# Attention: value products on the 64 columns of the unit's own head, and the results of a tile in one PSUM bank

## The reference, cut to what matters

```
s_loc = q @ k_window.T * scale (+ bias, mask);  s_ctx = q @ k_cache.T * scale
p     = softmax([s_loc, s_ctx] (, sink))
o     = p_loc @ v_window + p_ctx @ v_cache
```

## Time and profile before

| | |
|---|---|
| median of 3 runs | 4721.29 us (4719.97 to 4725.55) |
| profiled execution, its own time | 4717.61 us |
| its span, first to last instruction | 4715.8 us |
| mean granted TensorE clock | 0.906 |
| busy: PE, PEld, DVE, ACT, POOL | 3943.4, 3420.0, 1757.2, 866.7, 683.1 us |
| attention units, even layer | about 366 to 583 us |
| attention units, odd layer | about 2654 to 2922 us |

### The profile page before, as it was taken

The page is one execution under the profiler, slowest core; times in us unless marked ns, Lnnn a source line. Parts: engine busy times, 40 slices in busy tenths (PEclk is TensorE's granted clock), DMA queues, the critical chain, the costliest instruction groups (busy, mean ns, idle before and its releaser), DMA issues. The chain is left out here.

```text
span 4715.8 us, 62439 instructions
## 1 busy us (share of the span) xinstructions
PE 3943.4 (84%) x25842; PEld 3420.0 (73%) x25842; DVE 1757.2 (37%) x3337; ACT 866.7 (18%) x2008; POOL 683.1 (14%) x521
## 2 busy tenths in 40 slices
PE   4979978986769999996999597438886859999995
PEld 3976623444569999995999475338885659999995
DVE  3245541224531211123123454677876441121112
ACT  2113320001100110012111123424443100011001
POOL 2000110111100011002000000036651101001100
PEclk7988979997889999997999798768997979999998
DMA  4226412314547777773421402332223547777774
GB/s 151 89 82 233 148 67 98 137 40 149 201 148 268 261 266 264 268 257 117 116 89 67 108 8 76 102 88 60 73 65 130 190 154 264 268 259 267 266 268 155
DMA packets 353335, 744.94 MB, mean 158 GB/s; under 512 B 87432, under 2 KB 193559, under 8 KB 351976
## 3 DMA queue, kind: packets, MB, share of 16 engines
q1 hardware_dynamic: 333066, 683.15, 40.9%
q0 software_dynamic: 17392, 57.58, 4.5%
q10 hardware_dynamic: 2618, 0.40, 0.1%
HBM read 635.63 MB, written 106.10 MB: 157 GB/s over the span
## 5 line engine op out<-in xcount | busy, mean ns | idle before, releaser
L1826 PE MATMUL moe_b<-moe_xT,ffn_w 128*128 128x144 f32 x8192 | 1022.9, 287 | 0.0
L1826 PEld LDWEIGHTS moe_b<-moe_xT,ffn_w 128*128 128x128 f32 x8192 | 1012.7, 191 | 1.8
L1826 PE MATMUL moe_b<-moe_gu,ffn_w 128*128 128x144 f32 x4096 | 550.7, 288 | 0.0
L1826 PEld LDWEIGHTS moe_b<-moe_gu,ffn_w 128*128 128x128 f32 x4096 | 516.3, 190 | 4.8
L1871 DVE TENSOR_TENSOR moe_gu<-moe_sg,moe_b 128x144 f32<-128x144 f32 x256 | 77.9, 304 | 782.3 <-PE moe_b L1826 782.3
L1851 ACT ACTIVATE moe_yT<-moe_b 128x144 f32<-128x144 f32 x256 | 74.6, 291 | 1074.8 <-PE moe_b L1826 1074.8
L2380 PE MATMUL gdnc_a<-gdnc_T,gdnc_part 128*128 128x128 f32 x864 | 139.3, 318 | 156.7 <-POOL gdnc_part L2537 88.0
L1859 DVE TENSOR_SCALAR moe_xT<-moe_x,keep_coef 128x128 f32<-128x128 f32 (+1 forms) x544 | 154.7, 346 | 252.2 <-PE moe_x L1778 252.1
L2380 PEld LDWEIGHTS gdnc_a<-gdnc_T,gdnc_part 128*128 128x128 f32 x864 | 128.0, 229 | 162.7 <-POOL gdnc_part L2537 149.9
L1747 POOL DMA_INDIRECT scratch_x<-moe_ys,moe_slot x32 | 51.8, 1619 | 1260.7 <-DVE moe_yp L1881 1260.7
L297 PE MATMUL proj_mm<-proj_hT_low,proj_w_high 128*128 128x384 f32 x576 | 193.2, 335 | 0.0
(11 more groups left out here) (413 smaller groups left out, 6401.2 us busy)
## 6 DMA issues: line engine op xcount, KB each, us to landing
ffn_w<-moe_w_gate SPq DMA_DIRECT2D x32, 4096.0 KB, 15.8
ffn_w<-moe_w_up SPq DMA_DIRECT2D x32, 4096.0 KB, 13.9
ffn_w<-moe_w_down SPq DMA_DIRECT2D x32, 4096.0 KB, 15.7
attnrun_m_w<-w_ada SPq DMA_DIRECT2D x40, 1024.0 KB, 9.4
scratch_conv<-proj_zf POOLq DMA_DIRECT2D x24, 512.0 KB, 3.0
scratch_tm<-proj_tm SPq DMA_DIRECT2D x45, 208.0 KB, 1.9
proj_w_raw<-even_w_in SPq DMA_DIRECT2D x24, 384.0 KB, 4.2
scratch_spec<-filt_res SPq DMA_DIRECT2D x36, 256.0 KB, 2.1
```

The lines of the kernel that those rows point to most:

```text
L1826: mm = nc.tensor.matmul(bk[(m * FC + f) % 3][:, 0:SLOTS], w[m][:, k, f * P:(f + 1) * P], src[:, k, :], start=k == 0, stop=k == KD - 1)
```

## The change

The value tiles that stream are cut to the 64 columns of the unit's own head, in the keys' values (`tok`) and in the cached ones (`cv`). The result tensor `po` becomes 8 x 64 float32, one bank in place of two. Since the heads' results now lie side by side, VectorE scales all eight with one instruction of 512 elements in place of two of 256. The number, the order and the waits of TensorE's instructions stay.

```
-        po = s.ps("po", [P, 8, P])
+        po = s.ps("po", [P, 8, HD])
...
-            at = P * plan.kv_chunk(h)
-            tiles = [tok[:, k, v_at + at:v_at + at + P] for k in keys]
+            at = P * plan.kv_chunk(h) + HD * plan.chunk_half(h)[1]
+            tiles = [tok[:, k, v_at + at:v_at + at + HD] for k in keys]
             if cached:
-                tiles = [cv[:, at:at + P]] + tiles if even else tiles + [cv[:, at:at + P]]
+                tiles = [cv[:, at:at + HD]] + tiles if even else tiles + [cv[:, at:at + HD]]
...
-                for half in range(2):
-                    if even:
-                        src, r, dst = po[:, 4 * half:4 * half + 4, 64 * half:64 * half + 64], rinv[:, g % 2, 4 * half:4 * half + 4], o_sb[:, g % 2, 4 * half:4 * half + 4, :]
-                    else:
-                        src, r, dst = po[:, half:8:2, 64 * half:64 * half + 64], rinv[:, g % 2, half:8:2], o_sb[:, g % 2, half:8:2, :]
-                    ins = nc.vector.tensor_tensor(dst, src, r.unsqueeze(2).broadcast_to([P, 4, HD]), ALU.mult)
-                ins.then_inc(o_done, 1)
+                nc.vector.tensor_tensor(o_sb[:, g % 2], po[:], rinv[:, g % 2, :].unsqueeze(2).broadcast_to([P, 8, HD]), ALU.mult).then_inc(o_done, 1)
```

## The result

The changed kernel takes 4891.59 us, the median of four runs (4890.37 to 4892.26); beside them the kernel before took 4720.63 us (4719.85 to 4725.55, four runs). The ratio is 1.036 with a 95% interval of 1.0342 to 1.0378: slower by 171 us. The forecast was 4900, its range 4865 to 4918. The profiled execution of the changed kernel took 4892.26 us, with a span of 4890.5 and a mean granted clock of 0.866 (before: 0.906).

What follows compares the result with a forecast made beforehand. TensorE's pace and granted clock were taken to bound both attention stages. V 0, scaling 0, odd layer +176 and even layer +4 gave +180 on 4717.6, so 4897.6, forecast 4900 after the runs' median offset; range 4865 to 4918.

Steps and rivals of the forecast that it cites:

- V's length: V products in both layers: weight loads set their pace, so 64 columns save 0, bounds -68 us and 0.
- the bound of -68 us: V in both layers: the saving if the spacing of its 1216 records halved as the columns do, 68 us.
- the rival of cheap narrow products: V in both layers: 64-column records need half the time; 4653 us if the clock holds; chance 0.02 with clock kept.
- the ends of groups: Odd layer, TensorE's wait at seven group ends: 1.75 us each at half clock, +12.3, bounds 0.85 and 2.56 each.
- Bank and scaling: One bank and one VectorE scaling instruction for two: taken as 0, bounds -2.7 us and 0.
- The odd layer's clock: Odd layer stays at half clock to its end: tiles 0 to 7 take 419.4 us, +172.8; with the prompt +176.
- The prompt: Odd layer's last V block and prompt units, about half at full clock before: about +3 us.
- The even layer: Even layer: clock rises slightly later, +2 us, and may fall earlier in the prompt units, +2; sum +4.
- The clock holds: Rival, whole kernel: clock follows how long TensorE is occupied, so no change, 4721 us or 1 to 3 less; chance 0.08.
- Comes back in some groups: Rival, odd layer: full clock returns in one to seven groups, about 20 us saved each, 4880 to 4760; chance 0.09.

Runs made afterwards that it cites:

- experiment 1: Kernel before with only the V products narrowed to 64 columns in both layers, two banks and two scaling instructions kept: 4894.59 us.
- experiment 4: Changed kernel plus unread 512-column products in the odd layer: in set-up, first scores and group ends 4708.6 us; start only 4868.68; without set-up 4705.18.
- experiment 5: Changed kernel plus unread 64-column products, four in place of each 512-column one, behind the odd layer's first scores and at its group ends: 4916.0 us.
- Experiment 3: Kernel before with V streaming 96 or 80 of the 128 columns in both layers, two banks kept: 4765.48 us and 4870.44 us.
- experiment 4, start only: Changed kernel plus unread 512-column products in the odd layer, 35 in its set-up and 2 behind its first scores, none at group ends: 4868.68 us.

## Why the prediction was right

- *V's length: nothing.* Nearly. The spacing of the weight loads stayed at 0.21 us at half clock (eight in 1.78) and the same at full (four in 0.53), and the bound of -68 us, with the rival of cheap narrow products, falls. What the step left out is that a block as a whole gets shorter, by 0.11 us at half clock (1.98 for 2.09, 2.40 for the earlier trace rows's 2.51) and by 0.05 at full. That the saving lies behind the last record, where no further load of the block follows, is read from the spacing, not measured apart. In the odd layer it is 63 blocks, -6.9 us; with +1.8 for the ends of groups (below) it makes nearly all of 413.85 for 419.4.
- *Bank and scaling: nothing.* Shown by experiment 1: 413.86 us with two banks and two instructions, 413.85 with one.
- *The odd layer's clock.* The cause held, and experiments 1, 4 and 5 show it: narrow products alone lose it, wide products beside them bring it back, and the same inserts made of thin ones don't. The units were 5.82 and 6.89 us, forecast 5.90 and 6.99. A group's end was 1.96 to 2.02 and not 1.75, +1.8 in seven. The reason given was right, only the copy is waited for; the middle of the bounds had no working behind it and came out 0.25 too low. The two slips partly cancel, which is luck: +167.3 for +172.8. The prompt gave +2.5 for +3.
- *The even layer.* Forecast +4, measured +0.8. The clock rose 391 us into the program, 4.7 later than before (1.6 of these from ahead of the layer), inside the first modulation block as forecast: that block stands at 0.50 until 390.8. The late start cost +1.3 us (forecast +2). Once up, the clock held until the prompt, and over these units the changed kernel gained 2.4, most of what their 59 V blocks, shorter by 0.05 us each, would give (an estimate). It fell some us behind 574, in the prompt's units, where it had lasted to 584 before, and that cost +1.8 (forecast +2). So both clock terms came out about as forecast, and the step was too high because it had no term for the shorter blocks.
- *The reading of the rivals.* "The clock holds" is ruled out for this change, and experiment 5 rules out its reason: occupied time doesn't decide. "Comes back in some groups" was the right mechanism at another width. The sum of the profile was +180 and it is +174.7; 4.2 of these lie in stages that the change doesn't touch, so what answers to the forecast is +170.5.

What was argued better than it was known: that 64 columns are below what brings the clock back rested on the even layer's first 18.8 us and a few rises in the odd one. Experiment 3 shows how narrow the ground was: at 80 columns the clock came back once, and at 96 in most groups, which the rows of before could not have told.

What stays open: how much stream it takes (the runs show 64, 80, 96 and 128 columns and two kinds of inserts, no law), and which of the scores and transposes count for how much. The set-up's transposes raised the clock by themselves, while the even layer's first 18.8 us, with V at 128 columns, didn't. A kernel with narrow products and less weight loading wasn't tried.

## What to carry to other kernels

Columns that look wasted can be what keeps TensorE at its full clock: where products are paced by their weight loads, narrowing the stream saves little of each block (here 0.05 to 0.11 us), and can cost the clock (here 167 us). Before such an edit, look at the granted clock by stretch, at what the engine did just before each rise, and at whether anything wide is left in the stage. If the clock is at half in a stage that is bound by TensorE, try a few unread wide products where it starts and in its waits: 20 of them took the changed kernel from 4891.6 to 4701.3 us, and below the kernel before.

## What was not expected of the hardware

- TensorE can be busy for 430.19 us out of 430.19 and be granted 0.50 throughout (experiment 5).
- The same units can keep a full clock and fail to bring it back: eight narrow units ran at 1.00 behind the inserts (31.5 us with no fall), while some 50 narrow units behind the fall, 353 us, stayed at 0.50 (experiment 4, start only). That doesn't show that keeping takes less than raising, for at full clock the same units come faster: 202 records in 31.5 us, 6.4 a microsecond, against 1235 in 353, 3.5.
- With two products of 512 columns put behind the first two score blocks, the clock rose at 2658.6 us, while they ran, where in the kernel before all of the 15.8 us from 2654 to 2669.8 stood at 0.50.
- A wait for another engine can be shorter at half clock than at full: 1.15 us for 2.09 at a group's end, since TensorE then comes behind ScalarE's exponential and not ahead of it.
